# The order of the three matmuls of a split product, and the placement of the gated activations in SBUF

## The reference

```python
act = gelu(x @ u.T)              # [256 tokens, 16384], u and v are [16384, 1024]
out = (gate * act) @ v           # gate is zero but for the chosen 8 x 16 experts of a token
```

## The kernel before, in words

| tiles | before | after |
|---|---|---|
| `wH`, `wL` (all four buffers), `ring` | 0 | 0 |
| `hnH`, `hnL` and the arena's split rows `ff_a*`, `att_OT*`, `mem*`, `ycat*`, `pr_h*`, `od_h*`, `od_y*`, `ml_n*` | 192 (64 below) | 192 |
| `wgtH`, `wgtL`, `act_in`, `sq`, `onehot` | 0 | 224 (32 below) |
| `act_out`, `vec` | 192 | 224 |
| `con` (identity, ones), `iww` | 224 | 0 |

## Time and profile before

### The profile page before, as it was taken

One profiled execution on the slowest core, in us unless ns is written; L12 is line 12 of the kernel. 1 busy time (PEld: TensorE's weight loads), 2 busy tenths in 40 slices (PEclk: granted clock), 3 DMA queues, 4 the chain that ended last, 5 costly groups with the idle time before them and its releaser, 6 DMA issues.

```text
span 2811.2 us, 57248 instructions
## 1 busy us (share of the span) xinstructions
PE 2714.5 (97%) x19552; PEld 2544.1 (90%) x19552; DVE 2053.1 (73%) x4430; ACT 1454.5 (52%) x2378; POOL 177.8 (6%) x141
## 2 busy tenths in 40 slices
PE   7999999999999999989999999999999989999998
PEld 6999899999988888979998999988888889999998
DVE  8557997886566667876699888567776877666665
ACT  5455345444555555555544444455555565446544
POOL 0004000000000000000374000000000100000000
PEclk9999999999999999999999999999999999999999
DMA  5445566455766665424456555676666525563454
GB/s 190 176 157 184 204 215 213 174 182 195 261 242 242 242 242 179 149 78 165 165 182 217 191 172 183 218 258 242 242 242 242 187 81 182 190 230 117 177 184 178
DMA packets 140451, 546.19 MB, mean 194 GB/s; under 512 B 15784, under 2 KB 81592, under 8 KB 83616
## 3 DMA queue, kind: packets, MB, share of 16 engines
q1 hardware_dynamic: 63216, 455.38, 44.8%
q10 hardware_dynamic: 73728, 67.14, 7.4%
q0 software_dynamic: 3376, 21.88, 2.0%
HBM read 505.53 MB, written 40.91 MB: 194 GB/s over the span
## 4 chain that ended last, share of the span: by engine, by line
PE 78%; DVE 15%; DMA 2%; ACT 2%; issue 2%; DVEq 0%; ACTq 0%; SPq 0%
PE bank L796 23%; PE bank L797 23%; PE bank L798 23%; PE bank L1016 4%; DVE wL L551 4%; DMA ring<-in_w_stream 2%; PE bank L917 1%; ACT wH L540 1%; PE bank L937 1%; DVE pr_eq L1969 1%; DVE pr_eq L1971 1%; DVE pr_m L1973 1%; PE bank L928 1%; DVE pr_m L1924 0%; DVE pr_i L1924 0%
## 5 line engine op out<-in xcount | busy, mean ns | idle before, releaser
L551 DVE TENSOR_TENSOR wL<-ring,wH 128x1024 fp32r<-128x1024 f32 x809 | 988.1, 1224 | 605.5 <-ACT wH L540 602.5
L540 ACT ACTIVATE wH<-ring 128x1024 fp32r<-128x1024 f32 x864 | 907.3, 1055 | 423.2 <-DMA ring<-in_w_stream 252.6
L796 PE MATMUL bank<-hnH,wH 128*128 128x256 f32 x3528 | 1003.3, 284 | 34.5 <-DVE wL L551 26.6
L797 PE MATMUL bank<-hnL,wH 128*128 128x256 f32 x3528 | 984.0, 279 | 0.0
L798 PE MATMUL bank<-hnH,wL 128*128 128x256 f32 x3528 | 983.5, 279 | 0.0
L796 PEld LDWEIGHTS bank<-hnH,wH 128*128 128x128 f32 x3528 | 667.5, 189 | 45.7 <-issue 22.9
L797 PEld LDWEIGHTS bank<-hnL,wH 128*128 128x128 f32 x3528 | 667.2, 189 | 0.5 <-issue 0.2
L798 PEld LDWEIGHTS bank<-hnH,wL 128*128 128x128 f32 x3528 | 665.1, 189 | 0.0
L796 PE MATMUL bank<-wH,wgtH 128*128 128x512 f32 x1024 | 398.5, 389 | 0.3 <-DVE wgtL L2010 0.3
L798 PE MATMUL bank<-wH,wgtL 128*128 128x512 f32 x1024 | 398.4, 389 | 0.0
L797 PE MATMUL bank<-wL,wgtH 128*128 128x512 f32 x1024 | 398.3, 389 | 0.0
(11 more groups left out here) (411 smaller groups left out, 3535.3 us busy)
## 6 DMA issues: line engine op xcount, KB each, us to landing
ring<-in_w_stream SPq DMA_DIRECT2D x432, 1024.0 KB, 4.9
act_parked<-act_out ACTq DMA_DIRECT2D x256, 128.0 KB, 3.0
act_in<-act_parked ACTq DMA_DIRECT2D x256, 128.0 KB, 2.7
sw_bias<-in_c_swa POOLq DMA_DIRECT2D x1, 4096.0 KB, 15.7
relb_rows<-rel_table POOLq DMA_DIRECT2D x1, 2048.0 KB, 10.0
h_parked<-h POOLq DMA_DIRECT2D x2, 1024.0 KB, 6.3
h_back<-h_parked POOLq DMA_DIRECT2D x2, 1024.0 KB, 6.2
od_relb<-relb_rows POOLq DMA_DIRECT2D x2, 1024.0 KB, 7.4
```

Of the source, the lines that this page charges most:

```text
L540: eng.activation(wH[:, b % NBUF, :], raw(b), ACT.Copy).then_inc(w_high, 1)
L551: eng.tensor_tensor(wL[:, b % NBUF, :], raw(b), wH[:, b % NBUF, :].bitcast(F32), ALU.subtract).then_inc(w_low, 1)
L796: pe.matmul(dst, lh, rh, start=start, stop=False, skip_group_check=True)
L797: pe.matmul(dst, lh, rl, start=False, stop=False, skip_group_check=True)
```

## The change

The second and third matmul of every split product change places, and the tiles that stand ahead of and behind `shared` are ordered otherwise. `rb` (32 bytes) now stands between the normed rows and `shared`, which shifts everything in `shared` by 32 bytes modulo 256. No instruction is added or removed, and no size changes.

```diff
+        small = sb("small", [P, 96])
+        snk = sb("snk", [P, 16])
+        hnH, hnL = sb("hnH", [P, DC, T], F32R), sb("hnL", [P, DC, T], F32R)
+        rb = sb("rb", [32, 8])
+
         (sq,) = stage(("sq", [DC, T], F32))
         (onehot,) = stage(("onehot", [16, P], F32))
         act_in, wgtH, wgtL = stage(("act_in", [4, T], F32), ("wgtH", [2, T], F32R), ("wgtL", [2, T], F32R))
         sb("shared", [P, DC * T])
-        small = sb("small", [P, 96])
-        snk = sb("snk", [P, 16])
-
-        hnH, hnL = sb("hnH", [P, DC, T], F32R), sb("hnL", [P, DC, T], F32R)
         act_out = sb("act_out", [P, 2, T])
...
         iww = sb("iww", [P, DC, 8])
-        rb = sb("rb", [32, 8])
...
                 pe.matmul(dst, lh, rh, start=start, stop=False, skip_group_check=True)
-                pe.matmul(dst, lh, rl, start=False, stop=False, skip_group_check=True)
-                return pe.matmul(dst, ll, rh, start=False, stop=stop, skip_group_check=True)
+                pe.matmul(dst, ll, rh, start=False, stop=False, skip_group_check=True)
+                return pe.matmul(dst, lh, rl, start=False, stop=stop, skip_group_check=True)
```

## The result

The changed kernel takes 2826.64 us (median of 10 runs, 2819.34 to 2831.75), the kernel before 2811.02 us (10 runs). The ratio is 1.0048, 95% interval [1.0034, 1.0062]: some 13.5 us slower (9.6 to 17.4 by the interval; the two medians lie 15.6 us apart). The profiled execution took 2822.38 us with a span of 2820.2, 9.0 us more than the one before.

What follows compares the result with a forecast made beforehand. The prediction took TensorE's matmul spacing to bound the kernel. Profiled execution 2813.5 us plus 0 each for count, order, down stage and transfers, with the median 3.0 above, gave 2816.5, written 2816; range 2790 to 2832.

Steps and rivals of the forecast that it cites:

- I take 0, the value of the row at offset 0: Second expert product (down stage), 3072 matmuls of 512 columns: shifting the gated activations costs 0, ends -31 and +15 us.
- exactly twice 113.3: Down stage: 226.7 ns doubles the 256-column spacing, so it belongs to the stream and placing the stationary tile gains nothing.
- The lower end, -31 us: Down stage: if 226.7 ns were a load-stream collision that 32 bytes end, 3072 x 10 ns would come back.
- slower, by the shift: Rival in `outs`: the down stage goes from 389 to 394 ns, +15 us, 2831; chance 0.11 for the full price.
- 32 below acts like 64 below: Down stage: the shifted gated activations would cost 5 ns a matmul, as the `token_major` rows at 64 below suggest.
- I take 0: Order of products, some 13,500 matmuls of 256 columns: the swap costs 0, bounds -31 and +31 us.
- The onehot matmuls keep both operands at one offset: One-hot matmuls: both operands shift together, so the shift costs 0 there.
- History seems to choose: 256-column matmuls: only history seems to choose between two spacings, 4.6 ns apart; argued for rival faster by order, chance 0.18.
- ±6 us from execution to execution: Whole kernel: the share of slow 256-column spacings varies between executions, counted as ±6 us.

Runs made afterwards that it cites:

- e3: Changed kernel with `rb` moved behind `shared`, so the gated activations lie 64 bytes below the weight tiles; single run 2828.05 us.
- e8: Changed kernel with `shared` placed ahead of `small`, so the gated activations lie 32 bytes above the weight tiles; single run 2832.92 us.
- e1: Kernel before with only the new order of products, placement unchanged; 2808.20 us against 2813.83, ratio 0.9985.
- e10: Changed kernel (new order) with an eight-element gap putting the gated activations back at offset 0, one-hot tiles still 32 below; 2802.21 us, ratio 0.9966 to the kernel before.
- e5: e2 (old order) with an eight-element gap putting the gated activations back at offset 0, one-hot tiles still 32 below; 2806.57 us against 2812.18 for the kernel before.
- e2: Kernel before with only the new placement (gated activations 32 below), products in the old order; 2823.03 us, ratio 1.0038.
- e12: e10 with only the low gated activations (`wgtL`) moved 32 bytes below the weight tiles, `wgtH` at 0; single run 2821.16 us.

## Why the prediction was wrong

**The frame was right.** TensorE bounds the kernel, the edits act through the spacing of its matmuls, and the counts, waits and transfers cost nothing: TensorE is busy 10.2 us longer in a span 9.0 us longer, and the landings went from 3.0 and 2.7 to 2.8 and 2.7 us. The measured 2826.64 us lies inside the stated range, but on the side that the forecast held unlikely. The base was also off: the 2816.46 us of three runs became 2811.02 over ten, so the forecast of 2816 stood 5 us nearer to the result than a sum from the better base would have.

**The step that failed** is "I take 0, the value of the row at offset 0", for the shift in the second expert product. The runs show 6.6 ns a matmul in its place: 3072 x 6.6 = 20.3 us. Two things were wrong in it. First, the bounds. I took the row at 64 below as the far end, though 32 lies between 0 and 64 only if the cost grows with the distance; e3 and e8 show that it does not, and the true value lay beyond both ends (395 ns against 389 and 394; 6.6 ns against 5). Second, the choice between the ends. The argument that 226.7 is a property of the stream (exactly twice 113.3) spoke against a gain, and no placement tried was below 226.7 ns, which agrees with it and doesn't prove it. But it says nothing about a loss, and there the only rows with another relation of weights and stationary tile were worse. With a gain unlikely and a loss in sight the value should have been on the side of the loss.

The lower end, -31 us, rests on plain float32 matmuls streaming 512 steps for 256 columns, which is read from their 216 ns; no run tested it.

**The rival that came** is "slower, by the shift", with its place (`outs` alone) and mechanism right, at 6.6 ns instead of 5 and with a chance of 0.11. Its sentence "32 below acts like 64 below" is wrong, and so is the 5 ns that it takes for 64. Those were read from the durations of the slowest lines of `token_major`; in the down stage itself 64 below costs 2.2 ns in spacing (e3), 7 us and not 15. Two errors nearly cancelled, so that its 15 us lie near the 20.3 measured is luck.

**The order.** "I take 0" holds within what was measured: with the placement of before, the down stage has 389 ns and the token loops 279 with either order; with the changed placement, 395 and 277 with either order. In the pairs that differ by nothing else the new order is 0.15% faster than the kernel before (e1), e10 is 0.16% under e5, and the changed kernel is 0.10% above e2 (by their ratios to the kernel before, from two sessions). The signs differ, and no stage carries the difference; whether the order is worth a few microseconds stays open. The test by which the prediction took 0, that one line of the three would carry an expensive pair, was weaker than it seemed: in the second down stage of e12 one tile of three is displaced, and the three lines lie within 2 ns.

**"The onehot matmuls keep both operands at one offset"**, costed at 0, missed 5.5 us of gain. The one-hot matmuls themselves didn't change (274 ns before and after); the products after them fell less often into the slow spacing. With it the sum is 20.3 - 5.5 = +14.8 us, against 13.5 measured (9.6 to 17.4).

**"History seems to choose"** the spacing is in part shown: the share of slow ones differs between profiles where no tile concerned was moved. The feed-forward products on `ff_aH` and `ff_aL` have a mean of 284, 283 and 283 ns in the kernel before and 277 in e2, with rows and weights at the same distance. This fits the ±6 us from execution to execution which the prediction counted, and runs of one kernel that lie 15 us apart. What sets it at each stage's start is not settled.

**The Trainium skill**, page "TensorE: Matmul & The Clock Gate", section "Step-by-step: what each phase is for", says that the two read ports are independent, so that a weight load takes nothing from the running matmul. The runs don't agree: 226.7 against 233.3 ns by the relation of the two tiles' addresses, and the stationary tile is read by the load alone. They don't show by what path the load reaches the matmul. The formula in its section "Back-to-back issue gap", which gives 215.8 ns for 512 columns and is called there the gap of an isolated matmul, was not reached by the products of any variant; 226.7 is the least mean measured with these operands at that width.

## What to carry to other kernels

Where weight loads run beside dense matmuls of fp32r operands, the addresses of the stationary and the streaming tile modulo 256 are worth 3% of the stage in this kernel: measure the spacing between starts for the pair, and keep the distance that the trace shows to be fast, here 0 for 512 streaming columns (and 16 below as well), and for 256 columns 64 rather than 32, where 0 wasn't tried. Don't interpolate between offsets. When tiles share a place, as the one-hot tiles and the gated activations do here, give each its own offset with a small gap; moving the place moves all of them, and one may win what another loses.

## What was not expected of the hardware

In the steady stretches the spacing takes few values: 113.3 and 117.9 ns for 256 columns at a distance of 64, 118.7 at 32, and for 512 columns 226.7 ns at 0 and 16, 233.3 at 32, 228.9 at 64 and 232.4 at 128. 226.7 and 233.3 are 34 and 35 times 6.67 ns, and 113.3 is 17 times; the other values are no such multiples, so no more than a coincidence is shown. A tile displaced by 32 bytes in one matmul of three slows one neighbour or both, and this differs between the two down stages of the same run (e12: 389 and 395 ns on L799). As with the two spacings of the 256-column products, the same placement has more than one steady pattern.
